# Three seams of a two-block transformer kernel: order of the output projection's chunks, squares by heads on ScalarE, and unread products at the norms

## What is computed

```python
h = rmsnorm(x, ln1)
proj = h @ w_in                                   # 1024 x 3592
y_a = gated_deltanet(...)                         # 4 heads of 128, columns 0 to 511
y_b = dilated_attention(...)                      # 8 heads of 64, columns 512 to 1023
x = x + concatenate([y_a, y_b]) @ w_out           # output projection of block 1
h = rmsnorm(x, ln2)
x = x + (silu(causal_dwconv(h @ w_gate)) * (h @ w_up)) @ w_down
x = rmsnorm(x, ln_f)
```

```python
y = diff_attention(h, ...)      # layer 0: 8 heads, v of 128; o = rms_norm(o, subln_g) * 0.8, then o @ w_o
y = chunked_attention(h, ...)   # layer 1: 16 heads of 64, then o @ w_o
x = x + g1 * y
x = x + g2 * grouped_moe(rms_norm(x) * (1 + sc2) + sh2, ...)
```

## Time and profile before

| | |
|---|---|
| median of 3 runs | 1262.27 us (1260.25 to 1263.25) |
| profiled execution | 1263.72 us, its span 1261.8 us |
| mean granted clock of PE | 0.972 |
| busy: PE, PEld, DVE, ACT, POOL | 1141.0, 765.5, 606.7, 441.7, 69.1 us |
| chain that ended last | PE 72%, DMA 14%, DVE 9%, ACT 3%, issue 1% |

### The profile page before, as it was taken

The page is one execution under the profiler, slowest core; times in us unless marked ns, Lnnn a source line. Parts: engine busy times, 40 slices in busy tenths (PEclk is TensorE's granted clock), DMA queues, the critical chain, the costliest instruction groups (busy, mean ns, idle before and its releaser), DMA issues.

```text
span 1261.8 us, 16821 instructions
## 1 busy us (share of the span) xinstructions
PE 1141.0 (90%) x6516; PEld 765.5 (61%) x6516; DVE 606.7 (48%) x1170; ACT 441.7 (35%) x770; POOL 69.1 (5%) x137
## 2 busy tenths in 40 slices
PE   5999979888999997996799999987999999999986
PEld 4677547578999995875563443323787863443422
DVE  3268456446666666647642323224773542323223
ACT  5344512236444556536340110103654640110200
POOL 2111232100000000000000000000000000000000
PEclk9899989988999999998899999999999999999999
DMA  9998897635677772573079999997576279999995
GB/s 292 361 290 264 298 351 265 240 117 165 180 229 227 221 226 70 198 266 134 34 304 405 412 413 414 414 414 301 189 244 256 71 275 413 412 412 414 414 413 209
DMA packets 162955, 354.23 MB, mean 281 GB/s; under 512 B 9912, under 2 KB 78776, under 8 KB 162752
## 3 DMA queue, kind: packets, MB, share of 16 engines
q1 hardware_dynamic: 146864, 296.04, 64.2%
q0 software_dynamic: 16000, 57.16, 12.9%
q10 hardware_dynamic: 16, 0.02, 0.0%
HBM read 352.12 MB, written 7.36 MB: 285 GB/s over the span
## 4 chain that ended last, share of the span: by engine, by line
PE 72%; DMA 14%; DVE 9%; ACT 3%; issue 1%; POOL 0%; SPq 0%; ACTq 0%; DVEq 0%
PE bank L534 35%; PE bank L1066 12%; DMA ering<-in_moe_w_up 9%; PE bank L1077 8%; DMA ering<-in_ada_w 3%; PE bank L481 3%; PE bank L1034 3%; DMA wraw<-in_w_in 2%; PE bank L683 1%; PE bank L816 1%; DVE wlo L524 1%; PE bank L1723 1%; PE bank L1715 1%; PE bank L1726 1%; PE bank L1138 1%
## 5 line engine op out<-in xcount | busy, mean ns | idle before, releaser
L524 DVE TENSOR_TENSOR wlo<-wraw,whi 128x1024 fp32r<-128x1024 f32 x150 | 179.6, 1222 | 73.9 <-ACT whi L520 71.7
L520 ACT ACTIVATE whi<-wraw 128x1024 fp32r<-128x1024 f32 x150 | 153.9, 1054 | 75.2 <-PE bank L534 54.1
L534 PE MATMUL bank<-a_hi,whi 128*128 128x256 f32 x512 | 148.7, 290 | 3.2 <-DVE wlo L524 2.1
L534 PE MATMUL bank<-a_lo,whi 128*128 128x256 f32 x512 | 146.5, 286 | 0.0
L534 PE MATMUL bank<-a_hi,wlo 128*128 128x256 f32 x512 | 146.4, 286 | 0.0
L1066 PE MATMUL bank<-ering,work 128*64 128x512 f32 x592 | 134.3, 596 | 11.9 <-DMA ering<-in_moe_w_up 10.5
L534 PEld LDWEIGHTS bank<-a_hi,whi 128*128 128x128 f32 x512 | 99.9, 195 | 17.6 <-issue 15.6
L1267 DVE TENSOR_TENSOR work<-work,bank 128x512 f32<-128x512 f32 x16 | 11.0, 687 | 206.4 <-PE bank L1066 206.4
L534 PE MATMUL bank<-whi,a_hi 128*128 128x512 f32 x256 | 102.1, 399 | 2.7 <-DVE a_lo L737 2.7
L1066 PEld LDWEIGHTS bank<-ering,work 128*64 128x64 f32 x592 | 41.1, 137 | 102.7 <-issue 78.7
L1175 ACT ACTIVATE o_hi<-work 128x512 fp32r<-128x512 f32 x32 | 20.2, 630 | 236.0 <-DVE work L1235 235.5
(11 more groups left out here) (305 smaller groups left out, 1869.8 us busy)
## 6 DMA issues: line engine op xcount, KB each, us to landing
ering<-in_moe_w_down SPq DMA_DIRECT2D x44, 1024.0 KB, 18.3
ering<-in_moe_w_up SPq DMA_DIRECT2D x42, 1024.0 KB, 18.2
ering<-in_ada_w POOLq DMA_DIRECT2D x80, 512.0 KB, 6.0
ering<-in_moe_w_gate SPq DMA_DIRECT2D x32, 1024.0 KB, 18.2
work<-in_moe_w_gate SPq DMA_DIRECT2D x16, 1024.0 KB, 16.5
wraw<-in_w_in SPq DMA_DIRECT2D x28, 512.0 KB, 8.1
wraw<-in_a_w_qkv SPq DMA_DIRECT2D x24, 512.0 KB, 4.7
work<-in_moe_w_down SPq DMA_DIRECT2D x12, 1024.0 KB, 18.4
```

What stands on the lines that cost most here:

```text
L520: nc.scalar.activation(w_hi(c), wraw[:, c % RING, :], ACT.Copy).then_inc(w_hi_done, 1)
L524: nc.vector.tensor_tensor(w_lo(u[0]), wraw[:, u[0] % RING, :], w_hi(u[0]).bitcast(F32), ALU.subtract).then_inc(w_lo_done, 1)
L534: mm = nc.tensor.matmul(out_ap, l, r, start=first and n == 0, stop=last and n == len(terms) - 1)
```

## The change

- `w_out` is loaded with row chunks 4 to 7 first, and PE multiplies in this order. Turn 1 is cut in two: the banks of chunks 4 to 7 (`EARLY`) wait only for the local attention and are transposed right behind the last head products; the banks of chunks 0 to 3 (`LATE`) wait for `y_done` and are transposed behind the first two chunks' products. ACT makes the early high parts between its two roots, DVE the early low parts ahead of its scaling. PSUM banks are dealt anew: the last head products go to bank 0 and wait for `os_done`.
- Unread products: 18 behind the modulation columns ahead of turn 2, 11 behind the modulation rows in both layers, 10 ahead of turn 4 in layer 0.
- Differential attention's squares go to ACT, two instructions a head with their sum: heads 0 to 4 between attention's instructions, heads 5 to 7 behind the first splits of the projection's weights. The DVE product and reduction are gone. DVE scales in halves of four heads, and turn 4's first two banks wait only for the first half.

```diff
+OUT_ORDER = (4, 5, 6, 7, 0, 1, 2, 3)
 BUSY_WO = 8
+BUSY_NORM = 18
+BUSY_MOD = 11
+BUSY_Y = 10
...
-        TURN_BANK = {3: 4, 6: 4}
+        TURN_BANK = {1: (0, 2, 1, 3), 3: (4, 5, 6, 7), 6: (4, 5, 6, 7)}
+        TURN_ORDER = {1: (2, 3, 0, 1)}
+        EARLY, LATE = (2, 3), (0, 1)
...
-            load_square(a["w_out"][0], U_WOUT)
+            for n, k in enumerate(OUT_ORDER):
+                load_unit(sp, (U_WOUT + n, None, 0), a["w_out"][0][k * P:(k + 1) * P, :])
...
             pe.wait_ge(fin_copied, 3)
-            heads(psum[4], lambda h: aqk[1][:, h, :], lambda h: v1[:, h, :], fin_ps)
-
-            turn_pe(pe, 1, y_done, 2)
+            pe.wait_ge(os_done, 1)
+            heads(psum[0], lambda h: aqk[1][:, h, :], lambda h: v1[:, h, :], fin_ps)
+
+            turn_pe(pe, 1, att_y, SWA_H, banks=EARLY)
             pe.wait_ge(acol_done, 4)
...
-            square(U_WOUT, 1)
+            for n, k in enumerate(OUT_ORDER):
+                if n == 2:
+                    turn_pe(pe, 1, y_done, 2, banks=LATE)
+                if n == 0:
+
+                    pe.wait_ge(a_lo_done, 4 * HL[1] + 2)
+                chunk_ready(pe, 1, k)
+                unit_rows(pe, (U_WOUT + n, None, 0), a_hi[:, k, :], a_lo[:, k, :], psum[4:8], n == 0, n == KC - 1)
             mod_columns(psum[3])
+            busy(psum[0], BUSY_NORM)
...
                                      start=True, stop=True).then_inc(mod_ps, 1)
+                busy(psum[4], BUSY_MOD)
                 turn = 3 + 3 * l
...
                 if l == 0:
-                    turn_pe(pe, 4, y_done, 4)
+                    busy(psum[0], BUSY_Y)
+                    turn_pe(pe, 4, y_done, 6, halves=4)
...
                 rms(act, os_done, c + 1, or_done, M_OR + 4 * c, M_OS + 4 * c, 4, P)
-            act.wait_ge(ada_used, ADA_N)
-            turn_hi(act, 1, U_WOUT, vec[:, V_Y1:V_Y1 + 8])
+                if c == 1:
+                    act.wait_ge(ada_used, ADA_N)
+                turn_hi(act, 1, U_WOUT, vec[:, V_Y1:V_Y1 + 8], (EARLY, LATE)[c])
...
-                attention_act(act, 1 + l)
+                def squares(n):
+
+                    act.wait_ge(att_y, ATT_U[1] + n + 1)
+                    if n >= 2:
+                        act.wait_ge(os_done, 2 + n - 1)
+                    for t in range(T):
+                        ins = nc.scalar.activation(wk(3584 + P * (2 * (n % 2) + t), P), hn[:, t, n * P:(n + 1) * P], ACT.Square,
+                                                   accum_out=sm[:, M_OS + 8 * t + n:M_OS + 8 * t + n + 1])
+                    ins.then_inc(os_done, 1)
+
+                attention_act(act, 1 + l, lambda i: squares(i - 4) if l == 0 and i >= 4 else None)
                 splits(U_WO[l] + 2)
                 if l == 0:
+                    for n in range(A_H - 3, A_H):
+                        squares(n)
                     warm(ACT.Sqrt)
-                    rms(act, os_done, 3, or_done, M_OR, M_OS, 16, P)
+                    rms(act, os_done, 2 + A_H, or_done, M_OR, M_OS, 16, P)
...
             out_norm(1, osc[1])
             dve.wait_ge(z_evac, 2 * T)
+            turn_lo(dve, 1, vec[:, V_Y1:V_Y1 + 8], EARLY)
             for c in range(2):
                 invert(dve, or_done, c + 1, M_OR + 4 * c, 4)
...
                     dve.wait_ge(att_y, ATT_U[2])
-                    tmp = wk(2048, T, D)
-                    link(nc.vector.tensor_tensor(tmp, hn[:, :, :], hn[:, :, :], ALU.mult))
-                    nc.vector.tensor_reduce(sm[:, M_OS:M_OS + 16], tmp.rearrange("p t (h d) -> p (t h) d", d=P), AX.X,
-                                            ALU.add).then_inc(os_done, 1)
                     splits(U_WO[0] + 1)
                     invert(dve, or_done, 3, M_OR, 16)
-                    for t in range(T):
-                        v = hn[:, t, :].rearrange("p (h d) -> p h d", d=P)
-                        nc.vector.tensor_tensor(v, v, bc(M_OR + 8 * t, 8, P), ALU.mult).then_inc(y_done, 1)
+                    for half in range(2):
+                        for t in range(T):
+                            v = hn[:, t, half * HALF:(half + 1) * HALF].rearrange("p (h d) -> p h d", d=P)
+                            nc.vector.tensor_tensor(v, v, bc(M_OR + 8 * t + 4 * half, 4, P), ALU.mult).then_inc(y_done, 1)
```

## The result

The changed kernel takes 1256.28 us in the median of 20 runs (1252.45 to 1262.81), the kernel before, beside it on the same chip, 1262.09 (20 runs, 1256.21 to 1265.22). The ratio is 0.9958, with an interval of 0.9946 to 0.9970: 5.3 us less, between 3.8 and 6.8. The two traces therefore differ by more than the kernels do, 8.9 us.

The account below looks back on a forecast made before the run. The prediction took TensorE product streams to bound the kernel, with only the idle seams and slow clock behind them open to gain: 3.5 + 0.9 + 0 - 1.8 + 4.5 = 7.1 us off 1262.27 gives 1255.2, range 1251.5 to 1260.0.

Parts of the forecast that it names:

- N: Norm behind the delta net's output projection: 18 unread products keep the clock up, gaining 0.9 us.
- M1: Modulation rows ahead of layer 1's QKV: no idle time covers 11 unread products, costing 1.8 us.
- A: Delta net's end before the output projection: local attention's chunks first, half the old slow stretch left, gaining 3.5 us.
- D: Differential attention's end: squares on ACT, scaling in halves, one short clock fall, gaining 4.5 us.
- (2): Rival: the clock never falls at the two attention ends, A and D; 1252.7 us, chance 0.17.
- M0: Modulation rows ahead of layer 0's QKV: idle time covers 11 unread products, bringing 0.
- (3): Rival: in the seams the clock falls as before and unread products run at half clock; 1260.3 us, chance 0.11.
- (4): Rival: layer 0's expert loads start from something D doesn't move, so D is lost; 1259.7 us, chance 0.06.
- (5): Rival: differential attention's Square isn't in Exp's table set, so ACT makes seven extra loads; 1265.2 us, chance 0.04.
- (1): The forecast itself, whole kernel: all terms as stated, 1255.2 us, own range 1253 to 1258, chance 0.62.

Follow-up runs that it names:

- e12: The changed kernel itself, timed and profiled again beside e10 and e11 on one chip; 1256.18 us, ratio 0.995.
- e3: The kernel before with the three groups of unread products alone, in the old order; 1264.44 us, ratio 1.003.
- e6: e4 with squares, Sqrt table and root ahead of ACT's two weight splits, and DVE's split behind its scaling; 1255.13 us, ratio 0.9945.
- e9: The kernel before with only the 18 unread products behind the modulation columns added; 1264.41 us, ratio 1.0015.
- e4: The changed kernel without the 11 unread products ahead of layer 1's QKV; 1255.46 us, ratio 0.9952.
- e7: e4 with an extra unread Square of 1280 columns per head on ACT; 1266.14 us in a single run.
- e8: e4 with both layers' router constant rows moved from the feed-forward stream into seam N, five unread products left there; 1251.49 us, ratio 0.9908.
- e11: e10 with 11 unread products behind seam A's early transposes; 1247.41 us, ratio 0.989.
- e5: The changed kernel without any of its new unread products, order and squares kept; 1255.54 us, ratio 0.9954.
- e10: e6's order, router constant rows shared between seam N and layer 0's modulation seam instead of unread products there; 1249.09 us, ratio 0.9912.
- e2: The kernel before with only differential attention's squares on ACT and DVE's scaling in halves; 1259.65 us, ratio 0.9981.

## Why the prediction was right, and where it was not

The predicted time was 1255.2 us and the median is 1256.3; the sum of the terms was 7.1 us, the measured gain 5.3 (3.8 to 6.8). The sum was about 1.8 us too high and lies just outside that interval. The term that did most of it is N, and in part of the executions M1, both fillers. The terms that carried the forecast, A and D, hold. The four stretches A, N+F, M1 and D together are 5.5 us shorter than before in e12's trace and 3.8 in after's.

**A: right in mechanism and size** (predicted 3.5; measured 3.4 in eight of the nine traces with this order and no filler in it, 5.0 in the ninth). The timeline came out as it was written down: early high parts 1.55 us (1.65 predicted), early low parts 1.65, the wait for `os_done` at no cost, no wait for `y_done` behind 24 products. The choice of half the old slow stretch is what occurred, but it was a middle between two ends that no row showed, so that it was hit to the tenth is luck. The upper bound of 5.2, with none, is rival (2)'s half, and occurred once.

**N: the sign is wrong** (predicted +0.9, measured -0.5 to -2.0). The step that failed is the last one: "I expect the clock to stay up" is right for the seam (1.00 in 278 to 283 us, transposes 1.94 us), but the gain was read from the seam alone. The prediction tied the falls of the clock to long idle stretches, and so had none in the full stream, where one came. The gross gain was even of the predicted size: N+F is 206.63 us with one slow stretch of 3.4 us in it and 208.15 with twice as much, so such a stretch costs 1.5, and without any it would be 205.1, 1.0 less than before. But it always had one or two: net, N+F is 0.5 us longer than before in four traces (e3, e6, e9, e12) and 2.0 longer in three (after, e4, e7). The lower bound for this term, -1.5, assumed another cause (the filler itself at half clock), which didn't occur: 36 records took 4.26 us, the predicted 0.115 each.

**M0: right.** 0 predicted; 10.46 us in every trace with and without the filler, with 0.96 us idle left in front of the transposes instead of 3.42. **M1: mechanism right, size too small.** Predicted -1.8 with a bound of -2.0; measured 1.4 to 2.5 against traces in the same state, and between single traces up to 3.4 (after against before). The mis-sized term is the start: the trace of before had the modulation products at full clock (3.70 us) and the next instruction's earliest start was worked out from that; in after they took 5.40.

**D: right** (predicted 4.5; measured 4.2 in after's trace and 4.3 in e12's, 3.6 without the filler). Of it 3.1 us come ahead of the transposes in after (9.28 to 6.16 us behind the start of the last value products) and 3.9 in e12, the prediction had 3.3; attention's own stretch varies by some tenths. The clock fell once for 3.4 us, as taken. Two inputs were off without effect: a square is 0.29 us and not the 0.38 of the Exp it was bounded by, and the table, its call and the root followed each other without a gap. The Trainium skill (ScalarE: Activation LUTs, What ACT_TABLE_LOAD costs) has a drain of 1.38 us on top of a load of 1.28. This trace disagrees: the load starts at 595.82, the call at 597.11, the root at 597.22, and the instruction ahead of the load ends at 595.79. The prediction went by the trace, and was right to.

**The rivals.** (2), the clock never falling in A and D, occurred by half and once: in A in one of nine traces, in D in neither trace of the changed kernel. Behind attention there is no slow stretch in e8, whose D is the change's own (66.06, 4.7 us less than before), and none in e6 and e11, with the root moved forward. (3), fillers that don't work, was the one nearest to the miss, but by another mechanism than it described: they ran at full pitch and held the clock where they stood, and the slow stretch came later. As a judgement on the fillers (together worth nothing) it was right; its chance of 0.11 was low because it was priced as a failure of the seams, and A and D don't depend on fillers (e5 has 0.9954 without one). (4), experts that start from something else, is refuted: E0, measured from the first expert product, is 222.4 to 223.5 us in all traces, and the router ahead of it 16.84 in those in which it isn't slow, so what D gains is passed on in full. (5) is refuted by the timeline, and by the estimate at e7 it would have been over 4 us cheaper than priced, since the ring had room for about 0.9 us a head. One sum of the prediction doesn't come out: (1), (2) and half of (4) are 0.82, less a tail, and not 0.87, and the part of (3), half of (4) and the tail that is left for the same time is then nearer 0.15 than 0.10.

**What stays open.** Why filling seam N brings a slow stretch some 30 us later, at the constant rows, isn't settled. What the runs show is the pairing (filler and rows: seven of seven; rows alone: none of four; filler gone or cut to five products and rows elsewhere: none of e8, e10, e11). The rows alone aren't enough, the whole filler was never run without the rows in the stream, and the filler wasn't told apart from the rows' coming 1.0 us sooner. Nor is it settled why the routers are slow by 1.5 us in some traces: layer 0's in e3, e6, e7 and e9, layer 1's in e2, e3, e5, e6, e7, e8 and e11, with the same instructions in all of them. Layer 0's is slow only in traces that have the filler of N, in four of seven, which may be a further cost of it or chance.

## What to carry to other kernels

Take the gain from starting the product stream earlier (a part of the left side that is there already, a sum taken beside the work before) and from short small products moved out of a full stream into the idle seams; that is what held in every trace here that has it. The idle seam has to hold them: all 32 records in seam N cost 1.3 us there (e8), 16 in each of two seams nothing (e10). Unread products in a seam are to be judged by the whole time, with a look at the clock in the 50 us behind them: N's held it up in the seam, and it fell 30 us later in every trace with the rows there; and never put them where the trace shows no idle time to cover them, as ahead of layer 1's QKV. When a term depends on the clock, read the same place in more than one execution: here two profiles of one kernel differ by 1.5 to 1.7 us at each of three places.

## What was unexpected of the hardware

- **The clock fell with no idle time of PE ahead of it.** 308.9 to 315.7 us of the changed kernel has PE busy 6.80 of 6.80 us at 0.50, and the eight microseconds ahead of it 8.00 of 8.00 at 1.00. What was different shortly before the fall was 32 records of 16 columns that start 0.11 us apart, each with a weight load of its own (0.19 us). The profile gives each of them 0.26 us with a modelled end, so that "busy" here says little of how much PE works. The Trainium skill (TensorE: Matmul & The Clock Gate, Part 1: The HAM clock gate) has the lower level follow on an idle engine. This trace shows no idle time of PE in the eight microseconds ahead of the fall, so its busy share gave no sign of it.
- **Some falls come at the same place in nearly every trace.** Twelve of the fourteen traces have one at A: ten of them 5.1 to 5.5 us behind the start of the last head products, in the old order and the new, two at 6.0 and 6.2. In the four with the old seam N it comes 3.2 to 3.3 us behind the modulation columns. In the stretches compared here, slow stretches lasted 3.4, 6.8 or 10.2 us, nothing between.
- **Small products cost a full stream real time.** The 32 records took 3.48 us in the stream at full clock, and the stream became 3.3 us shorter when they left it (202.78 in e10 against 206.08 in e5); in the seams of e11 they took 2.86 and 1.85 us for half of them each, and cost nothing there.
- **A nearly full engine had room.** With the change's squares ACT is busy 8.75 of 10.50 us in 578.1 to 588.6 us (three heads), and the ring of attention kept its 3.51 us a head. 1.25 us more on ACT cost 0.36 of it.
